# Block 2's NSA units: causal mask added by TensorE, one maximum for both heads, exponentials that read the score banks

## What is computed

```python
s = jnp.einsum('bgqrd,bgqkd->bgrqk', qg, kb).astype(jnp.float32) * ATTN_SCALE
p = _masked_softmax(s, (kpos <= t[None, None, :, None])[:, :, None])
o_slc = jnp.einsum('bgrqk,bgqkd->bqgrd', p.astype(vb.dtype), vb)
...
o_nsa = o_cmp * gt[..., 0:1] + o_slc * gt[..., 1:2] + o_win * gt[..., 2:3]
```

## Time and profile before

| | us |
|---|---|
| median of 3 executions | 2613.24 (2607.68 to 2614.02) |
| the profiled execution | 2615.02 |
| its span, first to last instruction | 2612.9 |
| block 2's 52 units, first scores to last result part | 148.3 (1981.9 to 2130.2 us) |

### The profile page before, as it was taken

One profiled execution on the slowest core, in us unless ns is written; L12 is line 12 of the kernel. 1 busy time (PEld: TensorE's weight loads), 2 busy tenths in 40 slices (PEclk: granted clock), 3 DMA queues, 4 the chain that ended last, 5 costly groups with the idle time before them and its releaser, 6 DMA issues. The chain is left out here.

```text
span 2612.9 us, 33470 instructions
## 1 busy us (share of the span) xinstructions
PE 2471.3 (95%) x12473; PEld 1971.6 (75%) x12473; DVE 1262.5 (48%) x2342; ACT 953.0 (36%) x1490; POOL 1229.6 (47%) x1594
## 2 busy tenths in 40 slices
PE   7999989999999999998999999999888899999998
PEld 5788657888888778865788887887565567788887
DVE  6983543353335567445343224246678954512211
ACT  5333432332222432233333222244336764523322
POOL 3443324555556644433365555556323333455553
PEclk9999889999999999989999999999988999999999
DMA  4232212332222232221233322222220001232222
GB/s 153 84 84 78 65 50 80 105 109 102 97 97 91 95 98 74 78 73 57 65 107 115 102 92 97 95 91 87 97 77 17 1 23 51 82 104 97 90 97 88
DMA packets 80289, 218.60 MB, mean 84 GB/s; under 512 B 15744, under 2 KB 25344, under 8 KB 79616
## 3 DMA queue, kind: packets, MB, share of 16 engines
q1 hardware_dynamic: 60912, 200.96, 23.2%
q10 hardware_dynamic: 19216, 15.51, 2.1%
HBM read 207.78 MB, written 2.10 MB: 80 GB/s over the span
## 5 line engine op out<-in xcount | busy, mean ns | idle before, releaser
L906 POOL TENSOR_TENSOR w_lo<-w_raw,w_hi 128x256 fp32r<-128x256 f32 (+1 forms) x1482 | 1158.2, 812 | 1257.1 <-ACT w_hi L1471 1257.0
L967 PE MATMUL psG<-h_hi,w_hi 128*128 128x512 f32 x1880 | 760.4, 404 | 11.8 <-POOL h_lo L913 3.7
L968 PE MATMUL psG<-h_lo,w_hi 128*128 128x512 f32 x1880 | 742.5, 395 | 0.0
L969 PE MATMUL psG<-h_hi,w_lo 128*128 128x512 f32 x1880 | 741.9, 395 | 0.0
L1471 ACT ACTIVATE w_hi<-w_raw 128x1024 fp32r<-128x1024 f32 (+4 forms) x417 | 404.0, 969 | 500.6 <-PE psG L969 485.0
L967 PEld LDWEIGHTS psG<-h_hi,w_hi 128*128 128x128 f32 x1880 | 360.7, 192 | 106.1 <-issue 19.9
L969 PEld LDWEIGHTS psG<-h_hi,w_lo 128*128 128x128 f32 x1880 | 359.1, 191 | 77.9
L968 PEld LDWEIGHTS psG<-h_lo,w_hi 128*128 128x128 f32 x1880 | 361.3, 192 | 75.0 <-issue 2.7
L967 PE MATMUL psG<-m_hi,w_hi 128*128 128x512 f32 x800 | 311.6, 390 | 1.1 <-DVE m_lo L1951 1.1
L969 PE MATMUL psG<-m_hi,w_lo 128*128 128x512 f32 x800 | 311.3, 389 | 0.0
L968 PE MATMUL psG<-m_lo,w_hi 128*128 128x512 f32 x800 | 311.2, 389 | 0.0
(11 more groups left out here) (348 smaller groups left out, 2728.0 us busy)
## 6 DMA issues: line engine op xcount, KB each, us to landing
w_raw<-wstream SPq DMA_DIRECT2D x327, 512.0 KB, 3.3
w_raw<-wstream SPq DMA_DIRECT2D x64, 256.0 KB, 2.6
w_raw<-wstream SPq DMA_DIRECT2D x16, 384.0 KB, 2.9
work_b<-work_b ACTq DMA_DIRECT2D x16, 256.0 KB, 3.6
work_b<-cmpw ACTq DMA_DIRECT2D x2, 2048.0 KB, 8.1
x<-xT SPq DMA_DIRECT2D x4, 512.0 KB, 7.9
small_work<-ssmp ACTq DMA_DIRECT2D x8, 256.0 KB, 2.7
outT<-x SPq DMA_DIRECT2D x1, 2048.0 KB, 6.3
```

Of the source, the lines that this page charges most:

```text
L906: ins = pool.tensor_tensor(lo[:, c], w[:, c], hi[:, c].bitcast(F32), ALU.subtract)
L967: pe.matmul(out, whi, hi, start=(k == 0), stop=False)
L968: pe.matmul(out, whi, lo, start=False, stop=False)
L969: ins = pe.matmul(out, wlo, hi, start=False, stop=(k == K - 1))
```

## The change

Block 2's slc and win units (`in_banks`) change as follows; cmp and DSA keep their operations.

- PE: two more products for a unit add the mask of the last 128 columns onto the scores in the banks (identity times the 128x128 mask). `s_sc` is raised after them.
- DVE: one `tensor_reduce` over both heads' banks in place of the two fused operations; nothing is written to `p`. DVE's wait for the transposes of unit n-4 is moved to ACT for these units.
- ACT: the exponentials read the banks, not `p`.
- All kinds, cmp and DSA too: the scores of unit n wait for `s_exp` of unit n-2 in place of `s_masked`.
- `ahead` is 2 in place of 3 for all of them.

```diff
         def ahead(u):
 
-            return {"sw": 1, "x": 2}.get(u["kind"], 3)
+            return {"sw": 1}.get(u["kind"], 2)
...
                 before = n if kind == "sw" else n - 1
                 if kind == "x":
                     pe.wait_ge(s_exp, before)
+                elif kind != "sw":
+                    pe.wait_ge(s_exp, before)
                 elif before > 0:
                     pe.wait_ge(s_masked, before)
...
-                    ins = pe.matmul(out[:, a], lhs, rhs, start=True, stop=True)
+                    ins = pe.matmul(out[:, a], lhs, rhs, start=True, stop=not in_banks(u))
+                if in_banks(u):
+                    W = u["W"]
+                    for a in range(2):
+                        ins = pe.matmul(out[:, a, W - P:W], ident, con("mk", SEQ)[:, SEQ - P:SEQ], start=False, stop=True)
                 ins.then_inc(s_sc, 1)
...
-                src = score_banks(u) if kind == "x" else p
+                src = score_banks(u) if kind == "x" or in_banks(u) else p
+                if in_banks(u):
+                    act.wait_ge(s_tr, n - 3)
                 do(act.activation(p[:, 0], src[:, 0], ACT.Exp, bias=st[:, 2:3], scale=scale[0], accum_out=st[:, 4:5]))
...
-                ring = 4 if kind == "x" else ahead(u) + 1
-                if n >= ring:
+                ring = 2 if kind == "sw" else 4
+                if n >= ring and not in_banks(u):
                     dve.wait_ge(s_tr, n - ring + 1)
...
-                if kind == "x":
+                if kind == "x" or in_banks(u):
                     do(dve.tensor_reduce(st[:, 0:2], src, AX_X, ALU.max), s_masked)
```

More of the change, by code:

```diff
@@ L664, in narrow, with in_banks @@
             return u["kind"] in ("sw", "x")
+        def in_banks(u):
+            return u["kind"] in ("slc", "win")
         def ahead(u):
-            return {"sw": 1, "x": 2}.get(u["kind"], 3)
+            return {"sw": 1}.get(u["kind"], 2)
         def stats(u):
```

## The result

The changed kernel takes 2713.7 us (median of 4 runs, 2711.7 to 2722.0) against 2611.8 us for the kernel before (median of 4, 2607.7 to 2614.0): ratio 1.0393, 95% interval 1.0375 to 1.0410. The forecast was 2692, range 2675 to 2730. In all comparisons one execution of 4918.5 us, of the kernel before with another order on DVE, is left out; nothing here explains it.

What follows compares the result with a forecast made beforehand. Block 2 had PE, DVE and ACT near their limit; the new wait closes a ring. Turns 204.1, start 17.0 and end 5.8 make 226.9 us in place of 148.3, so 2692 us, range 2675 to 2730.

Steps and rivals of the forecast that it cites:

- The ring: Block 2: exponentials(i+1), scores(i+3), transposes(i), copy(i), exponentials(i+2) form a loop, one unit a turn; 5.38 us against 3.11 at W = 512.
- DVE's saving: One reduction replaces two fused operations and read-outs: 0.20 us in each of 32 units, 6.4 us, all hidden by the ring.
- The sum of the turns: Block 2's ring turns over all units, less start and end parts, plus 3.7 us for cmp units: 204.1 us.
- The mask: PE's two added products per unit, four instructions: 0.26 us, between nothing and 0.32.
- The nearest row: Row pricing the mask on PE: the values, 16 instructions of 128 columns in 1.03 us, 0.064 each.
- The clock: PE's granted clock stays at 1.00 behind the start of block 2's stretch; below 0.9 would refute the forecast.
- The rival: PE's idle times in the ring make the clock swing, half the time at the lower level: 45 us more, 2738; 12%.
- the forecast's own 89 us: Scores, mask, filler and transposes on PE, about 89 us of the ring, take twice as long if the clock falls.
- start, to the end of the third unit's exponentials: Block 2's start, from the first scores: 17.0 us, with part of it at half clock.
- end, behind the last exponentials: From the last exponentials' end to block 2's last result: stays at about 5.8 us.
- the cross-attention's two units ahead: The cross-attention has the same wait without the ring's cost, because PE there issues only scores of unit i+2 in step i.
- the likeliest case: The ring binds and the clock holds: 2692 us, range 2675 to 2712, chance 83%.

Runs made afterwards that it cites:

- the wait alone: Kernel before with one edit: block 2's scores of unit n wait for s_exp of unit n-2 in place of s_masked; 2702.7 us, ratio 1.0353.
- the two runs with PE kept busy: Changed kernel with three unread products behind each step's values, 2702.0 us; the same also without the mask products, 2685.3 us.
- the kernel before with the result first: Kernel before, `ahead` three, with DVE's order result of i-2, maximum of i+2+1, scaling of i+1: 2615.6 us, ratio 1.0006.
- the filler: Changed kernel with three unread products of 128x256 behind the values of each step: 2702.0 us, ratio 1.0341.
- Opening the first: Changed kernel with PE's scores two units ahead instead of three: 2658.0 us, ratio 1.0177.
- the three rings open: Changed kernel, `ahead` two, scores one unit later, DVE's order result, maximum, scaling: 2628.4 us, ratio 1.0055.
- the maximum first: Kernel before, `ahead` 3, with DVE's order maximum, scaling, result: 2611.1 us, ratio 1.0001.

## Why the prediction was right, and where it was not

**The ring** was right, and it is the larger part: the wait alone costs 3.5%. Its signs were there as forecast: idle time of PE ended by the exponentials, all engines less than full, DVE's saving of no use.

**The sum of the turns** was right but for one term. With the clock held, the turns from the end of the third unit's exponentials to that of the last's take 213.8 us; the forecast said 204.1. That it agrees this closely, once the mask is put right, is partly luck: a DSA unit at W = 384 takes 4.04 us, not 4.38, and a cmp unit and the one behind it take longer than forecast (at W = 384 4.04 + 5.59 us against 2.95, 4.87 with the mask put right, and at most 1.3 more). The products added to hold the clock also lengthen some turns at W = 128; with the shorter of the two kernels' turns for each unit the sum is 210.6.

**The mask was mis-sized.** The forecast took 0.26 us a unit, with 0.32 as upper bound; the timeline shows 0.55 and the two runs with PE kept busy give 0.52. The additional 0.29 for 32 units is 9.3 us (7.4 with the 0.49 by which the turns of W = 512 shrink without it), and 204.1 + 9.3 = 213.4 against the 213.8. The nearest row was chosen wrongly: the values of the earlier trace rows stream 128 columns, as the mask does, but their loaded tile has 64 columns (128x64 in the loads' shapes), and the mask's has 128, like that of the transposes. Those stood in the same group of rows: 8 instructions in 1.02 us, 0.128 each, so 0.51 for four. The upper bound should have come from there. The page "TensorE: Matmul & The Clock Gate" of the Trainium skill, in "Part 2: What happens when you issue a matmul", says that the time of a weight load scales with the tile's column count; by it the transposes were the row to take, and the trace agrees (0.064 and 0.128 us).

**The clock** was the step that failed. "The granted clock stays at 1.00 behind the start" was wrong; it was 0.85, under the 0.9 that the forecast had named as refuting. The step that led there compared a single gap of 1.81 us, which the clock had withstood, with one turn's idle time of 1.3 to 1.9 us. The idle times themselves were forecast well (1.9 us at W = 512 and 2.6 at a cmp unit; 1.94 and 2.97 in the trace). Wrong was what they do: they come in every turn, PE is busy for 69% of the stretch (174.3 of 252.4), and a gap that held once doesn't bound what a row of them does. It doesn't even bound what one does. The idle time in the other rows was misread: with two levels a mean of 0.66 over 285 to 286 puts the fall at 285.3, not 285.7, and PE's last product before it ended at 284.0, so 1.3 us of idle time came before that fall. And in the kernel before with the result first, whose time is the same, the clock fell just behind a gap of 1.55 us, one unit further on than the gap of 1.81 that had left it up. A line of the kernel before, then two of that run:

```profile
285.00:285.50 0.50, 0.00 (x0) 0.00 (x0) 0.43 (x3) 0.47 (x2) 0.00 (x0) 0.81 0.78 303
```
```profile
2034.46 1.48 PE L1176 MATMUL psO<-work_b 128*64 128x128 f32 x12 [1.55 <-DVE h_lo L1951]
2034.50:2035.00 0.50, 0.50 (x6) 0.50 (x8) 0.47 (x3) 0.00 (x0) 0.00 (x0) 0.57 0.00 0
```

The section that the forecast cites, "A second HAM failure mode: psum-queue depth-cycling" on the page "TensorE: Matmul & The Clock Gate" of the Trainium skill, tells of a kernel whose frequent short idle times between groups of matmuls made the clock swing, and the trace agrees with 75.4 us at the lower level.

What was mis-sized too is the clock's price. The rival asked 45 us for it; the filler got 11.7 us back, and in the two traces the turns differ by 228.8 - 213.8 = 15.0 (18.2 against the 210.6 above; the end behind the last exponentials is 1.9 longer with the filler). It isn't that PE stood idle at the lower level: over the thirteen pieces of the stretch at that level PE was busy for 66.8 of 75.4 us.

```profile
sum 75.38, PE 66.75 PEld 43.54 DVE 33.02 ACT 21.62 POOL 14.37; mean PE 5.13 PEld 3.35 DVE 2.54 ACT 1.66 POOL 1.11
```

The rival took half of the ring's time to be at the lower level; of the turns' 228.8 us it was 64.2, 28%. By the forecast's own 89 us of PE's work in the ring that would be 25 us, an estimate. The rest of the difference wasn't taken apart; the values of unit i-1 aren't on the ring, and what they take longer comes out of PE's wait.

**The stretch, term by term**, the changed kernel's trace against the forecast (the 213.8 is that of the run with PE kept busy):

| | forecast | measured |
|---|---|---|
| start, to the end of the third unit's exponentials | 17.0 | 18.0 (1976.07 to 1994.06) |
| turns at full clock, mask at 0.26 | 204.1 | 204.5 (213.8 less 9.3) |
| mask, the rest of its price | 0 | 9.3 |
| lower clock in the turns | 0 | 15.0 |
| end, behind the last exponentials | 5.8 | 5.6 |
| sum | 226.9 | 252.4 |

**DVE and ACT.** The reduction of 1024 columns takes 1.22 us and the exponential of 512 columns from a bank 0.78, both as forecast from neighbouring forms. DVE is busy for 4.3 us less, not 6. The saving of 0.20 a unit counted gaps that aren't busy time, and it missed that the small multiplication behind the maximum takes longer behind the reduction: all 48 of them together 10.0 us in place of 8.4 (0.33 us in the turn at 2002.46).

**What was not looked for** is what lay behind the ring. The forecast asked whether DVE would be last within the ring's turn, and that was answered rightly, but it named the cross-attention's two units ahead as free of the cost. For the ring through ACT that holds. In these units the change also sets `ahead` to 2, and that closes the ring through DVE, which alone costs 54 us (2665.6). While the first ring binds, the second is hidden. Opening the first leaves 46 of the 102 us (2658.0), and 30 of these go once DVE's order is changed as well (2628.4).

One small slip: the forecast's terms for the upper end of the likeliest case add up to 2692 + 2 + 15 = 2709, not 2712. The measured 2713.7 lies above both, and both errors, mask and clock, went the same way. It is inside the stated range because that had been stretched toward the rival of the clock.

## The remaining 14 us

With the three rings open, the changed kernel stands 3.0 us above the old one with the same order on DVE and the same `ahead` (2628.4 and 2625.4); the two differ in PE's scores as well, two units ahead against three. The intervals of the two ratios overlap (1.0040 to 1.0070 and 1.0028 to 1.0062), so it isn't settled that this difference is more than nothing. The mask's 32 x 0.52 = 16.7 us on PE is thus nearly paid by what DVE and ACT save, or hidden beside them; which of the two wasn't tried. The other 11 us, from 2614.3 to 2625.4, come with `ahead` 2 (maxima and exponentials two units ahead, scores three); through which wait is open. No version was faster than the kernel before beyond the noise (2611.1 against 2611.8 us with the maximum first). In the kernel before PE is busy for 130.7 of the stretch's 148.6 us, and the change puts work on PE.

## To carry to other kernels

When a change moves a wait to a later event, follow the wait back through every engine's queue until it meets itself; divide the time of that loop by the number of units it advances. One unit a turn is a serial chain whatever the busy shares say, and behind the longest such loop another may stand, so walk each queue order again with the first one opened. Price a small matmul by a row whose loaded tile has the same number of columns, and don't take the clock to be safe because one gap was survived: here a shorter one, a unit further on in a kernel of the same time, was followed by a fall.

## What the runs showed of the hardware

- Taking work off a waiting PE can bring nothing: leaving out the mask's 64 products brought 2.5 us, inside the spread of the runs, while the clock could fall (120.2 us at the lower level without them, 75.4 with them), and 16.7 us with the clock held.
- Three unread products in each step, with which PE is busy for 48 us more, made the program 11.7 us faster in the one pair (2713.7 to 2702.0) and 25.9 us in the other (2711.2 to 2685.3).
- The length of one idle time of PE didn't decide whether the granted clock fell: it fell 1.3 us into an idle time (kernel before, 285.3 us), 0.1 us behind one of 1.55 (kernel before with the result first, 2034.6) and 0.5 us behind one of 2.97 (changed kernel, 2007.1); it stayed up through one of 1.81 (kernel before, 2034.5) and through two of 1.67 with PE kept busy otherwise.
- A waiting PE can stay at the lower level for long: without the mask's products the granted clock was 0.50 from 2141.2 to 2178.6 us, with PE busy for 28.7 of these 37.4 us.
